# Spreading one row of scalars over 128 partitions: TensorE transposes against two DMA hops

## The chip, the cores and the metric

The kernel runs on one core of a Trainium2 chip. The metric is the device time of one execution in microseconds; the kernel before takes 571.8 us (median of 3 runs, 571.37 to 571.92). "PE" is TensorE, "DVE" VectorE, "ACT" ScalarE, "SP" the queue engine that issues nearly all DMAs, "us" microseconds.

## What is computed

A decoder layer on 256 tokens of width 2048: a gated mixer of 8 differential-attention heads and 8 block-sparse heads, then cross-attention into a memory of 256 rows, each behind an RMSNorm and with a residual. Cut to what the change touches:

```
h = rmsnorm(x, norm_mix_g)                 # x * r_x * gain, r_x = rsqrt(mean(x^2) + eps), one per token
proj = h @ w_in                            # 2048 x 8192
lam = exp(sum(lq1 * lk1)) - exp(sum(lq2 * lk2)) + 0.2
logits = (q . k) * scale + alibi           # per head, causal
attn = softmax(logits of map 0) - lam * softmax(logits of map 1)    # differential heads
```

The kernel multiplies with the raw x (times the gain) and puts r_x in afterwards. For queries r_x is one value per partition (a token is a partition), so it is a column. Keys stand transposed, with tokens along the free axis, so they need r_x as a row of 256 values, the same on all 128 partitions: that is the tile r_row. In the same way -lambda, a single number, must stand on every partition: that is neg_lam.

## The kernel before

The input projection runs as 8 windows, one for each pair of heads, of 16 "halves" (n = 0 to 15). A half is 256 rows of a 512-column slab of weights: SP loads it (two DMAs of 256 KB, L466; 8 buffers, so the load of half h + 8 waits until DVE is done with half h), ACT rounds it to a high part (L898), DVE subtracts to get a low part (L1229, two halves ahead of PE), and PE does 12 matmuls of 512 columns with them (L629 to L631). Halves 0 to 7 give the queries and keys of the pair, halves 8 to 15 its values and gates. The attention of a pair is woven into this stream by the number n in the loops of every engine, and each engine does its instructions strictly in the order written.

Around the change, in window 0: at n = 8 ACT copies the finished query and key projection to SBUF (L1003) and SP turns it with two DMA transposes (L485, issued behind the first two loads of the next window). At n = 8 DVE also works out r_x (L1449 to L1276), spreads it along the free axis (L1452, the tile r_rows) and then works on lambda; lambda is finished at n = 9 (L1471). At n = 10 PE transposes r_rows (L741, two transposes) and multiplies a matrix of ones with the column that holds -lambda in its partition 0 and zeros elsewhere (L745). At n = 11 DVE copies both results out of PSUM (L1476, L1477). At n = 12 DVE first makes the low part of half 14 (L1229), then scales the keys by r_row (L1295) and makes the low parts of queries (L1301) and keys (L1301 again), the last behind ACT's high part of the keys (L1014). PE needs all of them for the scores, which stand behind half 13 (L693 to L699).

At the very start PE runs matmuls on a tile of ones (keep_busy, L639) while the first data arrive. That tile lies in the first half of r_row.

Of the kernel before, what the change touches and what calls it, by code (L numbers as in the profile page):

```python
# [30 lines left out]
P = 128  # L31
SEQ = 256
DM = 2048
NT = SEQ // P
# [67 lines left out]
WARM_UP = (5, 2)  # L102
# [2 lines left out]
Y_TURN_AT = 6  # L105
P_TURN_AT = (10, 11)
MEM_LOAD_AT = 14


class Slots:  # L110
# [23 lines left out]
def program(nc, x, mem, norm_mix_g, w_in, lambda_q1, lambda_k1, lambda_q2, lambda_k2,  # L134
            subln_g, w_out, norm_mem_g, mem_norm_g, w_q_mem, w_kv_mem, w_o_mem, final_g, out):
    with ExitStack() as ctx:
# [3 lines left out]
        def sem(name):  # L140
            return ctx.enter_context(nc.semaphore(name))
# [18 lines left out]
        r_row = sbuf("r_row", [P, SEQ])  # L160
        alibi = sbuf("alibi", [P, 2, SEQ])
        pool = sbuf("pool", [P, 9 * COLS])
        ident = sbuf("ident", [P, P])
# [30 lines left out]
        y_sb, at = carve(pool, at, NT, 2 * P)  # L194
        junk, at = carve(pool, at, COLS)
        assert at <= 9 * COLS

        r_rows = y_sb[:, :, 0:P]

        ones = r_row[:, 0:P]  # L200
        junk_row, _ = carve(pool, 0, DM)
# [124 lines left out]
        r_x_ready = sem("r_x_ready")  # L326
        lam_steps = sem("lam_steps")
        ones_ready = sem("ones_ready")
        lam_zeroed = sem("lam_zeroed")
        lam_made = sem("lam_made")  # L330
        lam_dots = sem("lam_dots")
        lam_exps = sem("lam_exps")
        lam_ready = sem("lam_ready")
        r_rows_ready = sem("r_rows_ready")
        r_row_made = sem("r_row_made")
        r_row_ready = sem("r_row_ready")
        qk_planes_ready = sem("qk_planes_ready")
        qk_turned = [sem("qk_turned0"), sem("qk_turned1")]
        qk_merged = sem("qk_merged")
# [116 lines left out]
        def _(sp):  # L456
# [38 lines left out]
            def turns(n, j, y_too=True):  # L495

                if n == QK_TURN_AT:
                    for t in range(NT):
                        turn_qk(j - 1, t)
                if n == Y_TURN_AT and y_too:  # L500
                    turn_y(j - 2)
                if n in P_TURN_AT:
                    turn_probabilities(j - 1, n - P_TURN_AT[0])
# [25 lines left out]
            for n in range(PAIR_HALVES):  # L529
                load_pair_half(DIFF, 1, 1, n)  # L530
                turns(n, 1, False)
            with sp.Fori(2, KIND_PAIRS) as j:
                for n in range(PAIR_HALVES):
                    load_pair_half(DIFF, j, j, n)
                    turns(n, j)
# [72 lines left out]
        def _(pe):  # L608
# [26 lines left out]
            def keep_busy(count):  # L635


                with pe.Fori(0, count):
                    pe.matmul(ps[:, 2, 0:P], ones, ones, start=True, stop=True)  # L639

            def transpose_gains():

# [79 lines left out]
            def pair_window(j, kind, first=False):  # L722

                for n in range(PAIR_HALVES):
                    within = n % (2 * NG)
                    if n == 0:
                        wait(pe, qk_planes_ready, 2 * j)
                    if n == PAIR_HALVES // 2:
                        if first:
                            pe.wait_ge(gainsT_ready, 3)  # L730
                        wait(pe, v_ready, 2 * j)
                    if first and n < PAIR_HALVES // 2:
                        first_half_group(n)
                    else:
                        half_group(PAIR_HALVES * j + n, n % SPLITS, (0, 1) if n < PAIR_HALVES // 2 else (2, 3),
                                   aT_hi, aT_lo, within * (GK // 2), within == 0, within == 2 * NG - 1)
                    if first:
                        if n == 10:
                            pe.wait_ge(r_rows_ready, 1)
                            for t in range(NT):  # L740
                                m = pe.transpose(ps[:, 6, t * P:(t + 1) * P], r_rows[:, t], ident[:, :])  # L741
                            m.then_inc(r_row_made, 1)
                            pe.wait_ge(ones_ready, 1)
                            pe.wait_ge(lam_ready, 2)
                            pe.matmul(ps[:, 6, SEQ:SEQ + 1], ones, neg_lam_row[:, :], start=True, stop=True  # L745
                                      ).then_inc(lam_made, 1)
                    else:
                        attend_values(n, j - 1, WINDOW)
                    attend_scores(n, j, kind)

# [4 lines left out]
            pe.transpose(ps[:, 3, 0:KO], mix_gain[:, :], ident[0:KO, 0:KO]).then_inc(gainsT_made, 1)  # L755
            transpose_rows(0)
            transpose_rows(1)
            keep_busy(WARM_UP[1])
            pair_window(0, DIFF, True)
            with pe.Fori(1, KIND_PAIRS) as j:  # L760
                pair_window(j, DIFF)
# [460 lines left out]
        def _(dve):  # L1222
# [198 lines left out]
                rsqrt(r, ms, newton[:, 0:NT], steps, extra + 1)  # L1421

            dve.memset(ones, 1.0).then_inc(ones_ready, 1)
            dve.memset(neg_lam_row, 0.0).then_inc(lam_zeroed, 1)
            dve.wait_ge(gainsT_made, 1)
            dve.tensor_copy(gainsT[:, 0:KO], ps[:, 3, 0:KO]).then_inc(gainsT_ready, 1)
            dve.wait_ge(gainsT_ready, 1)
# [17 lines left out]
            for n in range(2 * NG, PAIR_HALVES):  # L1445
                split_lo(n + 2, n + 2)
                if n == 8:
                    dve.wait_ge(x_summed, 2 * NT)
                    dve.tensor_reduce(x_sq, x_sq2, axis=AX.X, op=ALU.add).then_inc(x_total, 1)  # L1449
                    dve.wait_ge(x_total, 1)  # L1450
                    row_rms(x_sq, x_ms, r_x, r_x_steps, 0)
                    dve.tensor_copy(r_rows, r_x.unsqueeze(2).to_broadcast([P, NT, P])).then_inc(r_rows_ready, 1)  # L1452
                    for kind in (DIFF, MOBA):
                        dve.tensor_scalar(r_q[kind.name], r_x, kind.scale, None, ALU.mult).then_inc(r_q_ready, 1)
                    dve.tensor_scalar(neg_r_x, r_x, -1.0, None, ALU.mult).then_inc(r_x_ready, 1)
                if n == 8:
                    dve.wait_ge(lam_loaded, 64)
                    for i in range(2):
                        dve.tensor_tensor(lam_prod[0:1, i], lam_in[0:1, 2 * i], lam_in[0:1, 2 * i + 1], ALU.mult
                                          ).then_inc(lam_steps, 1)  # L1460
                    for i in range(2):
                        dve.wait_ge(lam_steps, i + 1)
                        dve.tensor_reduce(lam_dot[0:1, i:i + 1], lam_prod[0:1, i], axis=AX.X, op=ALU.add
                                          ).then_inc(lam_dots, 1)
                if n == 9:
                    dve.wait_ge(lam_exps, 1)
                    dve.wait_ge(lam_zeroed, 1)
                    dve.tensor_tensor(neg_lam_row[0:1, :], lam_exp[0:1, 1:2], lam_exp[0:1, 0:1], ALU.subtract
                                      ).then_inc(lam_ready, 1)
                    dve.wait_ge(lam_ready, 1)  # L1470
                    dve.tensor_scalar(neg_lam_row[0:1, :], neg_lam_row[0:1, :], -LAM_INIT, None, ALU.add  # L1471
                                      ).then_inc(lam_ready, 1)
                if n == 11:
                    dve.wait_ge(r_row_made, 1)
                    dve.wait_ge(lam_made, 1)
                    dve.tensor_copy(r_row[:, :], ps[:, 6, 0:SEQ]).then_inc(r_row_ready, 1)  # L1476
                    dve.tensor_copy(neg_lam, ps[:, 6, SEQ:SEQ + 1]).then_inc(r_row_ready, 1)  # L1477
                    dve.wait_ge(r_row_ready, 2)
                    dve.wait_ge(r_q_ready, 2)
                attend_scores(n, 0, DIFF)  # L1480
            with dve.Fori(1, KIND_PAIRS) as j:
# [157 lines left out]
```

## Time and profile before

| | us |
|---|---|
| median of 3 runs | 571.8 |
| the profiled execution | 571.67 |
| its span | 569.9 |
| PE busy | 561.0 (98%) |
| DVE busy | 427.5 (75%) |
| ACT busy | 407.8 (72%) |
| 16 DMA engines, busy share of queue 1 | 75.5% |

The span is the time from the first to the last instruction of the profiled execution; 1.8 us of its time lie outside. PE is busy nearly all the time, so only what keeps PE waiting, or adds work to it, lengthens the run. Matmuls overlap in the pipeline: a 512-column matmul is shown with 0.39 us, but one starts every 0.23 us, so starts are compared, not durations.

### The profile page before, as it was taken

How to read it: one execution, taken by the hardware profiler on the slowest of the kernel's cores; microseconds unless marked ns; L12 is line 12 of the kernel's file. 1: busy time of each engine (PE TensorE's matmuls, PEld its weight loads, DVE VectorE, ACT ScalarE, POOL GpSimd, SP SyncE). 2: the span in 40 equal slices, each digit the busy share in tenths (PEclk: the TensorE clock that was granted, in tenths of full speed). 3: DMA queues.
4: the chain of work that ended last, by engine and by line, in shares of the span. 5: the costliest groups of instructions: out<-in, count | busy, mean ns of one | idle time of the engine just before them, and what ended most of it. 6: DMA issues, size and time to landing. Idle time of an engine off the chain costs nothing.

```text
span 569.9 us, 8636 instructions
## 1 busy us (share of the span) xinstructions
PE 561.0 (98%) x2652; PEld 467.8 (82%) x2652; DVE 427.5 (75%) x720; ACT 407.8 (72%) x653; POOL 2.1 (0%) x26
## 2 busy tenths in 40 slices
PE   8999999999999999999999999999999999999994
PEld 7888888888888888888888888888888888888884
DVE  4779768778887876866756768667568886878985
ACT  5796876967868778776784784875498796856543
POOL 1000000000000000000000000000000000000000
PEclk9999999999999999999999999999999999999998
DMA  8996768668676776885975975769799987973903
GB/s 260 353 306 227 214 180 243 181 193 237 186 232 192 198 218 185 234 230 158 250 215 157 263 206 188 221 187 302 246 227 271 262 239 197 257 230 105 258 1 147
DMA packets 151236, 123.32 MB, mean 216 GB/s; under 512 B 66809, under 2 KB 133162, under 8 KB 150698
## 3 DMA queue, kind: packets, MB, share of 16 engines
q1 hardware_dynamic: 150890, 122.47, 75.5%
q10 hardware_dynamic: 320, 0.53, 0.3%
q8 instruction: 12, 0.20, 0.1%
q14 instruction: 14, 0.11, 0.1%
HBM read 105.93 MB, written 2.10 MB: 190 GB/s over the span
## 4 chain that ended last, share of the span: by engine, by line
PE 97%; DMA 1%; DVE 1%; ACT 0%; SPq 0%; issue 0%; ACTq 0%
PE ps L629 28%; PE ps L630 28%; PE ps L631 28%; PE ps L711 2%; PE ps L693 1%; PE ps L668 1%; PE ps L672 1%; PE ps L664 1%; PE ps L868 1%; PE ps L873 1%; PE ps L869 1%; DMA xs<-in_x 1%; PE ps L651 1%; PE ps L836 0%; PE ps L696 0%; PE ps L842 0%
## 5 line engine op out<-in xcount | busy, mean ns | idle before, releaser
L1229 DVE TENSOR_TENSOR w_lo<-w_raw,w_hi 128x1024 fp32r<-128x1024 f32 x183 | 222.7, 1223 | 104.7 <-ACT w_hi L898 102.7
L898 ACT ACTIVATE w_hi<-w_raw 128x1024 fp32r<-128x1024 f32 x183 | 192.5, 1057 | 81.8 <-PE ps L631 80.7
L629 PE MATMUL ps<-w_hi,aT 128*128 128x512 f32 x540 | 211.7, 392 | 0.0
L630 PE MATMUL ps<-w_lo,aT 128*128 128x512 f32 x540 | 210.3, 389 | 0.0
L631 PE MATMUL ps<-w_hi,aT 128*128 128x512 f32 x540 | 210.1, 389 | 0.0
L631 PEld LDWEIGHTS ps<-w_hi,aT 128*128 128x128 f32 x540 | 101.4, 188 | 21.2
L629 PEld LDWEIGHTS ps<-w_hi,aT 128*128 128x128 f32 x540 | 101.4, 188 | 20.9
L630 PEld LDWEIGHTS ps<-w_lo,aT 128*128 128x128 f32 x540 | 101.4, 188 | 20.4
L629 PE MATMUL ps<-w_hi,yT_hi 128*128 128x512 f32 x144 | 56.2, 390 | 0.0
L631 PE MATMUL ps<-w_hi,yT_lo 128*128 128x512 f32 x144 | 56.0, 389 | 0.0
L630 PE MATMUL ps<-w_lo,yT_hi 128*128 128x512 f32 x144 | 56.0, 389 | 0.0
L631 PEld LDWEIGHTS ps<-w_hi,yT_lo 128*128 128x128 f32 x144 | 27.0, 188 | 5.6
L629 PEld LDWEIGHTS ps<-w_hi,yT_hi 128*128 128x128 f32 x144 | 27.0, 188 | 5.6
L630 PEld LDWEIGHTS ps<-w_lo,yT_hi 128*128 128x128 f32 x144 | 27.0, 188 | 5.5
L1286 DVE RECIPROCAL pool<-pool 128x128 f32<-128x128 f32 x32 | 30.5, 953 | 1.1
L1003 ACT ACTIVATE mems<-ps 128x1024 uint16<-128x1024 uint16 x16 | 15.5, 1020 | 17.0 <-PE ps L631 16.9
L1024 ACT ACTIVATE pool<-pool,small 128x256 f32<-128x256 f32 (+1 forms) x48 | 21.3, 444 | 7.2 <-DVE small L1321 7.2
L973 ACT ACTIVATE pool<-mems 128x1024 uint16<-128x1024 uint16 x16 | 21.7, 1359 | 0.0
L1313 DVE SCALAR_TENSOR_TENSOR pool<-ps,small,alibi 128x256 f32<-128x256 f32 (+2 forms) x32 | 15.0, 511 | 5.8 <-PE ps L699 5.8
L964 ACT ACTIVATE probT<-mems 128x768 uint16<-128x768 uint16 x16 | 16.0, 1080 | 0.0
L1038 ACT ACTIVATE mems<-pool 128x768 uint16<-128x768 uint16 x16 | 13.3, 832 | 2.9 <-DVE pool L1338 2.9
L1203 ACT ACTIVATE pool<-xs 128x512 f32<-128x512 f32 (+1 forms) x8 | 4.8, 606 | 12.0 <-DVE xs L1574 12.0
(213 smaller groups left out, 580.0 us busy)
## 6 DMA issues: line engine op xcount, KB each, us to landing
w_raw<-in_w_in SPq DMA_DIRECT2D x251, 256.0 KB, 3.2
w_raw<-in_w_out SPq DMA_DIRECT2D x64, 256.0 KB, 3.9
w_raw<-in_w_kv_mem SPq DMA_DIRECT2D x32, 256.0 KB, 4.4
w_raw<-in_w_q_mem SPq DMA_DIRECT2D x16, 256.0 KB, 3.2
w_raw<-in_w_o_mem SPq DMA_DIRECT2D x16, 256.0 KB, 3.8
mems<-in_mem SPq DMA_DIRECT2D x1, 2048.0 KB, 9.6
xs<-in_x SPq DMA_DIRECT2D x3, 512.0 KB, 6.3
w_raw<-in_w_in SPq DMA_DIRECT2D x10, 128.0 KB, 4.6
```

The source lines that it names most:

```text
L629: pe.matmul(acc, hi[:, k0 + k, tok], w_hi[:, slot, k], start=first and k == 0, stop=False)
L630: pe.matmul(acc, hi[:, k0 + k, tok], w_lo[:, slot, k], start=False, stop=False)
L631: m = pe.matmul(acc, lo[:, k0 + k, tok], w_hi[:, slot, k], start=False, stop=last and k == GK // 2 - 1)
L898: act.activation(w_hi[:, i % SPLITS], raw, ACT.Copy).then_inc(hi_made, 1)
L964: act.activation(probT[:, u].rearrange("p i q -> p (i q)").bitcast(U16) .rearrange("p (c h) -> p h c", h=2), probT_planes[:, u].rearrange( ...
L973: act.activation(qkT_sb[:, :, t * P:(t + 1) * P].bitcast(U16) .rearrange("p i (q h) -> p h i q", h=2), qkT_planes[:, t].rearrange("p (h i ...
L1003: act.activation(qk_planes[:, t].rearrange("p (h c) -> p h c", h=2), ps[:, t, :].bitcast(U16).rearrange("p (c h) -> p h c", h=2), ACT.Copy ...
L1024: m = act.activation(prob_sb[:, u, c, cols], prob_sb[:, u, c, cols], ACT.Exp, bias=neg_max[:, u, t, c:c + 1], accum_out=exp_sum[:, c, u, t ...
L1038: act.activation(prob_planes[:, u].rearrange("p (h c) -> p h c", h=2), prob_sb[:, u, 0, :].bitcast(U16).rearrange("p (c h) -> p h c", h=2) ...
L1229: dve.tensor_tensor(lo, w_raw[:, i % RAW], hi.bitcast(F32), ALU.subtract).then_inc(lo_made, 1)
L1286: dve.reciprocal(s, s).then_inc(silu_steps, 1)
L1313: dve.scalar_tensor_tensor(prob_sb[:, u, 0:kind.maps, cols], banks[:, :, cols], r[:, t:t + 1], bias, ALU.mult, ALU.add).then_inc(logits_re ...
```

## The change

Two SP-issued hops take the place of the transposes. Behind the load of half 2 of window 1, SP waits for r_x and issues two DMAs that write the 256 values of r_x, four bytes from each partition, into one line of partition 0 (r_line, in the space of y_sb). Behind the load of half 3 it issues a DMA that writes -lambda from partition 0 to all partitions, waits until the line has landed and until PE has read the ones, and issues a DMA that reads the line 128 times and writes it to the 128 partitions of r_row. DVE at n = 11 waits for both landings instead of copying from PSUM. The loop of keep_busy is written out, so that its last matmul can signal.

```diff
--- before.py
+++ after.py
@@ -105,6 +105,8 @@
 Y_TURN_AT = 6
 P_TURN_AT = (10, 11)
 MEM_LOAD_AT = 14
+R_LINE_AT = 2
+R_ROW_AT = 3
 
 
 class Slots:
@@ -195,7 +197,7 @@
         junk, at = carve(pool, at, COLS)
         assert at <= 9 * COLS
 
-        r_rows = y_sb[:, :, 0:P]
+        r_line = y_sb[0:1, 0, :]
 
         ones = r_row[:, 0:P]
         junk_row, _ = carve(pool, 0, DM)
@@ -326,14 +328,13 @@
         r_x_ready = sem("r_x_ready")
         lam_steps = sem("lam_steps")
         ones_ready = sem("ones_ready")
-        lam_zeroed = sem("lam_zeroed")
-        lam_made = sem("lam_made")
+        ones_read = sem("ones_read")
         lam_dots = sem("lam_dots")
         lam_exps = sem("lam_exps")
         lam_ready = sem("lam_ready")
-        r_rows_ready = sem("r_rows_ready")
-        r_row_made = sem("r_row_made")
-        r_row_ready = sem("r_row_ready")
+        r_line_landed = sem("r_line_landed")
+        r_row_landed = sem("r_row_landed")
+        neg_lam_landed = sem("neg_lam_landed")
         qk_planes_ready = sem("qk_planes_ready")
         qk_turned = [sem("qk_turned0"), sem("qk_turned1")]
         qk_merged = sem("qk_merged")
@@ -529,6 +530,16 @@
             for n in range(PAIR_HALVES):
                 load_pair_half(DIFF, 1, 1, n)
                 turns(n, 1, False)
+                if n == R_LINE_AT:
+                    sp.wait_ge(r_x_ready, 1)
+                    for t in range(NT):
+                        sp.dma_start(r_line[:, t * P:(t + 1) * P], r_x[:, t:t + 1]).then_inc(r_line_landed, 16)
+                if n == R_ROW_AT:
+                    sp.wait_ge(lam_ready, 2)
+                    sp.dma_start(neg_lam, neg_lam_row[0:1, :].to_broadcast([1, P])).then_inc(neg_lam_landed, 16)
+                    sp.wait_ge(ones_read, 1)
+                    sp.wait_ge(r_line_landed, 32)
+                    sp.dma_start(r_row[:, :], r_line.unsqueeze(1).to_broadcast([1, P, SEQ])).then_inc(r_row_landed, 16)
             with sp.Fori(2, KIND_PAIRS) as j:
                 for n in range(PAIR_HALVES):
                     load_pair_half(DIFF, j, j, n)
@@ -635,8 +646,9 @@
             def keep_busy(count):
 
 
-                with pe.Fori(0, count):
-                    pe.matmul(ps[:, 2, 0:P], ones, ones, start=True, stop=True)
+                for _ in range(count):
+                    m = pe.matmul(ps[:, 2, 0:P], ones, ones, start=True, stop=True)
+                return m
 
             def transpose_gains():
 
@@ -734,17 +746,7 @@
                     else:
                         half_group(PAIR_HALVES * j + n, n % SPLITS, (0, 1) if n < PAIR_HALVES // 2 else (2, 3),
                                    aT_hi, aT_lo, within * (GK // 2), within == 0, within == 2 * NG - 1)
-                    if first:
-                        if n == 10:
-                            pe.wait_ge(r_rows_ready, 1)
-                            for t in range(NT):
-                                m = pe.transpose(ps[:, 6, t * P:(t + 1) * P], r_rows[:, t], ident[:, :])
-                            m.then_inc(r_row_made, 1)
-                            pe.wait_ge(ones_ready, 1)
-                            pe.wait_ge(lam_ready, 2)
-                            pe.matmul(ps[:, 6, SEQ:SEQ + 1], ones, neg_lam_row[:, :], start=True, stop=True
-                                      ).then_inc(lam_made, 1)
-                    else:
+                    if not first:
                         attend_values(n, j - 1, WINDOW)
                     attend_scores(n, j, kind)
 
@@ -755,7 +757,7 @@
             pe.transpose(ps[:, 3, 0:KO], mix_gain[:, :], ident[0:KO, 0:KO]).then_inc(gainsT_made, 1)
             transpose_rows(0)
             transpose_rows(1)
-            keep_busy(WARM_UP[1])
+            keep_busy(WARM_UP[1]).then_inc(ones_read, 1)
             pair_window(0, DIFF, True)
             with pe.Fori(1, KIND_PAIRS) as j:
                 pair_window(j, DIFF)
@@ -1421,7 +1423,6 @@
                 rsqrt(r, ms, newton[:, 0:NT], steps, extra + 1)
 
             dve.memset(ones, 1.0).then_inc(ones_ready, 1)
-            dve.memset(neg_lam_row, 0.0).then_inc(lam_zeroed, 1)
             dve.wait_ge(gainsT_made, 1)
             dve.tensor_copy(gainsT[:, 0:KO], ps[:, 3, 0:KO]).then_inc(gainsT_ready, 1)
             dve.wait_ge(gainsT_ready, 1)
@@ -1449,7 +1450,6 @@
                     dve.tensor_reduce(x_sq, x_sq2, axis=AX.X, op=ALU.add).then_inc(x_total, 1)
                     dve.wait_ge(x_total, 1)
                     row_rms(x_sq, x_ms, r_x, r_x_steps, 0)
-                    dve.tensor_copy(r_rows, r_x.unsqueeze(2).to_broadcast([P, NT, P])).then_inc(r_rows_ready, 1)
                     for kind in (DIFF, MOBA):
                         dve.tensor_scalar(r_q[kind.name], r_x, kind.scale, None, ALU.mult).then_inc(r_q_ready, 1)
                     dve.tensor_scalar(neg_r_x, r_x, -1.0, None, ALU.mult).then_inc(r_x_ready, 1)
@@ -1464,18 +1464,14 @@
                                           ).then_inc(lam_dots, 1)
                 if n == 9:
                     dve.wait_ge(lam_exps, 1)
-                    dve.wait_ge(lam_zeroed, 1)
                     dve.tensor_tensor(neg_lam_row[0:1, :], lam_exp[0:1, 1:2], lam_exp[0:1, 0:1], ALU.subtract
                                       ).then_inc(lam_ready, 1)
                     dve.wait_ge(lam_ready, 1)
                     dve.tensor_scalar(neg_lam_row[0:1, :], neg_lam_row[0:1, :], -LAM_INIT, None, ALU.add
                                       ).then_inc(lam_ready, 1)
                 if n == 11:
-                    dve.wait_ge(r_row_made, 1)
-                    dve.wait_ge(lam_made, 1)
-                    dve.tensor_copy(r_row[:, :], ps[:, 6, 0:SEQ]).then_inc(r_row_ready, 1)
-                    dve.tensor_copy(neg_lam, ps[:, 6, SEQ:SEQ + 1]).then_inc(r_row_ready, 1)
-                    dve.wait_ge(r_row_ready, 2)
+                    dve.wait_ge(r_row_landed, 16)
+                    dve.wait_ge(neg_lam_landed, 16)
                     dve.wait_ge(r_q_ready, 2)
                 attend_scores(n, 0, DIFF)
             with dve.Fori(1, KIND_PAIRS) as j:
```

On SP, after the two transposes of the query and key projection, where the loads of window 1 (L466, L467 in the new numbering) go on; before:

```order
L485 DMA_TRANSPOSE mems<-mems 128x8x128 [waits qk_planes_ready] x2
L466 DMA w_raw<-in_w_in 128x2x256 [waits lo_made]
L466 DMA w_raw<-in_w_in 128x2x256
L466 DMA w_raw<-in_w_in 128x2x256 [waits lo_made]
L466 DMA w_raw<-in_w_in 128x2x256
```

And the same place now:

```order
L486 DMA_TRANSPOSE mems<-mems 128x8x128 [waits qk_planes_ready] x2
L467 DMA w_raw<-in_w_in 128x2x256 [waits lo_made]
L467 DMA w_raw<-in_w_in 128x2x256
L536 DMA pool<-small 1x128x1 [waits r_x_ready]
L536 DMA pool<-small 1x128x1
L467 DMA w_raw<-in_w_in 128x2x256 [waits lo_made]
L467 DMA w_raw<-in_w_in 128x2x256
L539 DMA small<-small 128x1x1 [waits lam_ready]
L542 DMA r_row<-pool 128x1x256 [waits r_line_landed,ones_read]
L467 DMA w_raw<-in_w_in 128x2x256 [waits lo_made]
```

Four DMAs have come between the loads, and the last of them has a wait for the landing of the first two; the next load stands behind it.

On DVE, at n = 9 to 12 of window 0 (small holds -lambda, pool the queries and keys), before:

```order
L1471 TENSOR_SCALAR small<-small 1x1 [waits lam_ready]
L1229 TENSOR_TENSOR w_lo<-w_raw,w_hi 128x1024 [waits hi_made] x2
L1476 COPY r_row<-ps 128x256 [waits lam_made,r_row_made]
L1477 COPY small<-ps 128x1
L1229 TENSOR_TENSOR w_lo<-w_raw,w_hi 128x1024 [waits hi_made,r_q_ready,r_row_ready]
L1295 TENSOR_TENSOR pool<-pool,r_row 128x512 [waits qk_merged]
```

And now:

```order
L1470 TENSOR_SCALAR small<-small 1x1 [waits lam_ready]
L1231 TENSOR_TENSOR w_lo<-w_raw,w_hi 128x1024 [waits hi_made] x2
L1231 TENSOR_TENSOR w_lo<-w_raw,w_hi 128x1024 [waits r_q_ready,hi_made,neg_lam_landed,r_row_landed]
L1297 TENSOR_TENSOR pool<-pool,r_row 128x512 [waits qk_merged]
L1303 TENSOR_TENSOR qT_lo<-pool,qT_hi 128x512 [waits qkT_hi_ready]
```

The two copies are gone, and the low part of half 14 now stands behind the landings.

On PE, between half 10 and half 11 of window 0, before:

```order
L631 MATMUL ps<-w_hi,aT 128x512
L741 MATMUL ps<-ident,pool 128x128 [waits r_rows_ready]
L741 MATMUL ps<-ident,pool 128x128
L745 MATMUL ps<-small,r_row 128x1 [waits lam_ready,ones_ready]
L629 MATMUL ps<-w_hi,aT 128x512 [waits lo_made]
```

And now:

```order
L641 MATMUL ps<-w_lo,aT 128x512
L642 MATMUL ps<-w_hi,aT 128x512
L640 MATMUL ps<-w_hi,aT 128x512 [waits lo_made]
L641 MATMUL ps<-w_lo,aT 128x512
L642 MATMUL ps<-w_hi,aT 128x512
```

The halves follow each other with nothing between.

## Rows read from the trace of the kernel before

**Rows 1.** The page's shares of the chain that ended last, by engine

```profile
PE 97%; DMA 1%; DVE 1%; ACT 0%; SPq 0%; issue 0%; ACTq 0%
```

**Rows 2.** Waits of PE, whole span: us in total, times, longest

```profile
PE ps L639 <- DVE r_row L1423: 1.1, 1, 1.1
PE ps L664 <- ACT w_hi L915: 0.3, 1, 0.3
PE ps L651 <- DMA xs<-in_x: 0.2, 1, 0.2
```

**Rows 3.** Chain in order of time, 38 to 50 us: start, us, what

```profile
39.55 0.23 PE ps L631
39.79 0.22 PE ps L741 x2
...
40.12 0.34 PE ps L629
...
42.98 0.23 PE ps L629
...
48.42 0.55 PE ps L693 x6
```

**Rows 4.** Timeline of DVE, 38 to 50 us: start, us, instruction [idle before]

```profile
38.78 0.14 DVE L1471 TENSOR_SCALAR small<-small 1x1 f32<-1x1 f32 x1
...
42.85 0.42 DVE L1476 COPY r_row<-ps 128x256 f32<-128x256 f32 x1
...
43.97 1.22 DVE L1229 TENSOR_TENSOR w_lo<-w_raw,w_hi 128x1024 fp32r<-128x1024 f32 x1 [0.63 <-ACT w_hi L898]
45.11 0.68 DVE L1295 TENSOR_TENSOR pool<-pool,r_row 128x512 f32<-128x512 f32 x1
...
46.49 0.69 DVE L1301 TENSOR_TENSOR kT_parts<-pool,kT_parts 128x512 fp32r<-128x512 f32 x1
47.44 2.36 DVE L1229 TENSOR_TENSOR w_lo<-w_raw,w_hi 128x1024 fp32r<-128x1024 f32 x2 [0.26 <-ACT w_hi L898]
```

**Rows 5.** Timeline of SP, 38 to 40.3 us: start, time to issue

```profile
38.07 1.09 SPq L466 DMA_DIRECT2D w_raw<-in_w_in  x2
...
39.20 0.98 SPq L466 DMA_DIRECT2D w_raw<-in_w_in  x2
```

**Rows 6.** Line L466, the two loads issued at 39.2 and 39.7: issue, landing

```profile
L466 SPq DMA_DIRECT2D w_raw<-in_w_in x2: 469/469/469, 39.2 to 39.7; - x2
...
DMA to landing us min/median/max: 3.7/4.0/4.3
```

**Rows 7.** DMA issues of the whole span: KB each, median us to landing

```profile
w_raw<-in_final_g SPq DMA_DIRECT2D x1, 1024.0 KB, 6.8
...
out<-mems SPq DMA_DIRECT2D x2, 128.0 KB, 2.5
...
mix_gain<-in_norm_mix_g ACTq DMA_DIRECT2D x1, 8.0 KB, 1.9
```

**Rows 8.** Windows: length, busy PE, PEld, DVE, ACT, POOL, PE clock, DMA share, GB/s

```profile
557.00:558.00 1.00, 1.00 (x6) 0.84 (x5) 0.80 (x2) 0.06 (x1) 0.00 (x0) 1.00 1.09 451
...
564.50:565.00 0.50, 0.00 (x0) 0.00 (x0) 0.46 (x3) 0.24 (x1) 0.00 (x0) 0.72 0.00 0
565.00:570.00 5.00, 0.00 (x0) 0.00 (x0) 0.84 (x3) 1.09 (x2) 0.00 (x0) 0.50 0.58 210
```

**Rows 9.** Timeline of PE: its last matmuls, and the start

```profile
562.07 0.64 PE L873 MATMUL ps<-w_hi,cT_lo 128*128 128x256 f32 x4
...
1.13 2.53 PE L639 MATMUL ps<-r_row 128*128 128x128 f32 x10 [1.13 <-DVE r_row L1423]
...
3.90 1.11 PE L651 MATMUL ps<-ident,xs 128*128 128x128 f32 x4
...
5.82 0.70 PE L664 MATMUL ps<-w_hi,aT 128*128 128x512 f32 x2 [0.34 <-ACT w_hi L915]
...
17.30 1.03 PE L651 MATMUL ps<-ident,xs 128*128 128x128 f32 x8
```

## The prediction

> **What bounds the kernel now.** I read the chain that ended last first: 97% of it is PE [rows 1]. Then PE's waits: in the whole span it waits three times, 1.6 us in all, and all three are over by 8 us [rows 2]. From there to its last matmul PE never stands still. So the change can help by taking instructions off PE, and it can hurt by making PE wait where it does not now; DVE, ACT and the DMA queue count only through such a wait. I therefore looked next at the chain in order of time where window 0 spreads its scalars [rows 3], at what DVE does there [rows 4], at when SP can issue [rows 5] and at how long DMAs take to land [rows 6, 7].
>
> One measurement can tell a change of about 0.2%, here 1.14 us, from none. Below, "same" means within that.
>
> **What is removed.** PE loses two transposes and the small matmul. They start at 39.79; 12 matmuls after the first one behind them (40.12) PE is at 42.98. The pace of undisturbed matmuls is (48.42 - 42.98) / 24 = 0.227 us, so without the three PE would be at 39.55 + 13 x 0.227 = 42.50. They cost 0.48 us, and since PE is the chain, that is the full gain. DVE loses its two copies out of PSUM, which begin at 42.85, but it then idles 0.63 us for ACT's high part of half 14 anyway [rows 4], so they were hidden and their going gives nothing. The spreading copy at n = 8 and the memset at the start go too; DVE waits for ACT behind both, so they give nothing either.
>
> The warm-up loop that is written out changes instructions that PE runs while it waits for x: the first transposes of x cannot start before x lands, and PE waits again for x and for ACT after them [rows 2]. Its matmuls follow each other at the array's pace (10 records in 2.53 us [rows 9]), so nothing is gained inside the loop; a gain of a tenth of a us would end in the same wait for x. I take zero; both ends are within 0.1 us.
>
> **What is added, and where it sits.** The wait on the landings stands on DVE before the low part of half 14 (now at 43.97). Call S the time at which that subtraction starts. Behind it are the scaling of the keys (S + 1.14), and the low part of the keys, which started at 46.49 and took 0.69, so ends at S + 3.21 [rows 4]. PE starts the scores at once after that, say S + 3.3. Now S = 43.97, the operands are there at 47.3 and PE gets to the scores at 48.42: 1.1 us to spare. With 0.48 us taken off PE it gets there at 47.94. So PE does not wait if S is at most 44.6, the change breaks even at S = 45.1, and each us beyond is a us of the run. Behind that DVE has to make the low parts of halves 15 and 16; they start at 47.44 as a pair of 1.2 us each, and PE needs the first only after the scores and half 14, some 4 us after 48.42. PE is later by almost as much as DVE, so this cover holds and nothing is added there. On SP the next load waits for the landing of the line, some 2 us; the weights it brings are used 8 halves (over 20 us) later, so that is covered too.
>
> **When do the landings come?** SP has issued half 2 of window 1 by 39.16 [rows 5]; r_x is ready by then, since lambda, which is worked on after it, is done at 38.92 [rows 4]. Each issue takes 0.47 to 0.5 us. The two DMAs of the line go out at 39.2 and 39.7, the load of half 3 at 40.2 and 40.7, -lambda at 41.2, and SP is free to issue the row at 41.6 at the earliest. Two loads issued at exactly 39.2 and 39.7 before landed after 3.7 and 4.3 us [rows 6]; the shortest landing of the trace is 1.9 us [rows 7]. So the line is there between 41.6 and 44.0. Its own bytes are few, where each of those loads had 256 KB (0.7 us at the 350 GB/s of the stream) and the second had the first ahead: 4.3 - 1.4 is 2.9, and the 256 pieces of four bytes may take a few tenths. I take 3.3 us, landing at 43.0.
>
> The row then moves 128 KB inside SBUF. A store of 128 KB took 2.5 us, of which 0.3 to 0.4 us is data at the pace of all 16 engines, so about 2.1 us are fixed [rows 7]; the load issued before it adds perhaps 0.3. What remains is the data itself, and here the ends lie far apart. Every one of the 128 reads of 1 KB is of the same partition, and no row shows such a transfer.
> - If the 16 engines read it side by side, the data take 0.35 us. The row nearest to that is the gain vector, one row read 128 times from outside the core, 1 MB in 6.8 us with other loads ahead: repeating a source is not slow in itself [rows 7]. Then S = 43.0 + 2.1 + 0.3 + 0.35 = 45.8 (45 to 47 with a crowded queue).
> - If one partition gives no more than one engine's share, the data take 16 times as long. The fastest us in which data were read out of SBUF moved 451 GB/s, over 128 partitions, or 28.2 GB/s for a sixteenth [rows 8]; 131,072 bytes at that rate are 4.65 us. Then S = 43.0 + 2.1 + 0.3 + 4.65 = 50.05.
>
> I take the second. The transfer reads SBUF, as the store does, and the store's rate was reached with every partition giving a little; the gain vector was read from memory outside, which says nothing about one partition of SBUF.
>
> The Trainium skill has a rule for this, "SBUF — State Buffer", section "Door 1: The DMA port swizzle": partitions reach the DMA engines through 16 ports, eight partitions to a port, and a transfer confined to one port was measured at 27.6 GB/s. By that the 131,072 bytes would take 4.75 us, an estimate from the page that falls beside the 4.65 us worked out from the rows; no run here shows it yet.
>
> With S = 50.05 the scores start at 53.35 where they started at 48.42: +4.93 us, the 0.48 us already in it. PE then stands still from 47.94 to 53.35, 5.4 us.
>
> **The clock.** The last matmuls end at 562.71 [rows 9]. The granted clock was still 1.00 until 564.5, 0.72 over the next half us and 0.50 from 565 [rows 8]: it fell from 2.4 to 1.2 GHz at 564.7, two us after PE stopped. A stop of 5.4 us should make it fall too. What the slow level costs afterwards, the start shows: four transposes of x took 1.11 us at 3.90 and eight took 1.03 us at 17.30, half the pace, and by 5.82 the 512-column matmuls ran at full pace [rows 9], so slow running lasted from 1.13 to about 5. Half of such a stretch of 3.5 to 4 us is lost, less where part of it falls in the stop: between 0.8 and 2.0 us, I take 1.6.
>
> **Sum.** 571.67 (the profiled execution's own time, 0.13 below the median) + 4.93 + 1.6 = 578.2 us, 1.1% slower.
>
> **Rivals.**
> - The clock holds through the stop: 571.67 + 4.93 = 576.6. For it: the time of the fall is known from one place only. Against it: that place had a stop of two us, this one has 5.4.
> - One partition serves all engines at once. S = 45.8, scores at 49.1, +0.7 us: 572.4, and 573.6 if both landings meet a crowded queue (S = 47). This is the wait in its small form: PE stops for a us and a half and the clock stays. For it: the gain vector's row. Against it: no read of one partition in the trace.
> - Not slower: both hops land as in a quiet queue. Line at 41.6, row issued then and landed 2.5 us later, at 44.1. S is under 44.6, PE never waits, and the 0.48 us stay: 571.2. The point from which it decides is S = 45.1. For it: the 1.9 and 2.5 us of [rows 7]. Against it: the loads at the same moment took 3.7 and 4.3.
> - The small pieces are dear: the 256 four-byte writes, all to one partition, go one after the other and the line lands 2 us later than taken. This adds its 2 us to the first number: 580.2.
>
> **Chances.** The forecast (serial reads, clock falls) 0.53; serial reads with the clock held 0.12; the small pieces dear as well 0.07; side-by-side reads 0.22; both hops quiet 0.06. The first three, and a third of the fourth (S above 46.2), are slower by over 0.2%: 0.80. The rest of the fourth and most of the fifth are within it, 0.17. Faster would need 1.14 us where PE can give back only 0.48; I leave 0.03 for what I have not seen. The range runs from 572.2, which takes in most of the fourth case, to 580.0; the forecast's own would be 576.3 to 579.5.
>
> **What would show it.** In the profile after: the row's DMA issued at about 43 and landing 7 us later (2.5 to 3 if the rival is right); SP's next load behind it at about 43.5; DVE idle from 42.85 to about 50, released by that DMA; PE idle for 5 us before the first scores, released by DVE; the PE clock at 0.5 somewhere in 50 to 57 and matmul starts 0.45 us apart there; everything after at the old pace, with no wait on PE in windows 1 to 7. A landing under 3 us, or no gap on PE ahead of the scores, makes the forecast wrong; a gap with the clock at 1.00 behind it makes only its last term wrong.

## The result, and the profile after

| | before | after |
|---|---|---|
| median | 571.83 us (4 runs) | 580.09 us (4 runs, 579.51 to 580.64) |
| the profiled execution | 571.67 | 580.64 |
| its span | 569.9 | 578.8 |

The ratio is 1.0145, 95% interval 1.0133 to 1.0157: 8.3 us slower, where 6.5 were forecast and the range ended at 580.0. The way and the mechanism were as forecast; the size was short.

PE's waits in the whole span (us in total, times, longest), which answer to [rows 2]:

```profile
PE ps L705 <- DVE kT_parts L1303: 6.8, 1, 6.8
PE ps L650 <- DVE r_row L1425: 1.1, 1, 1.1
```

There is one new wait, and it is the one ahead of the first scores. The chain of window 0 in order of time (start, us, what) answers to [rows 3]:

```profile
38.58 0.57 SPq L467
...
39.71 0.59 SPq L536
...
40.34 4.64 DMA pool<-small
...
45.04 6.41 DMA r_row<-pool
...
51.47 1.22 DVE w_lo L1231
52.70 0.61 DVE pool L1297
...
53.33 0.64 ACT kT_parts L1016
...
54.00 0.70 DVE kT_parts L1303
...
54.74 1.01 PE ps L705 x4
...
57.14 0.72 PE ps L640
57.86 0.43 PE ps L641
...
60.42 0.35 PE ps L641
60.77 0.23 PE ps L642
```

Before, only PE stood here. Now the chain runs through SP, the line's DMA, the row's DMA, DVE, ACT and DVE again until PE has its scores at 54.74, where it began them at 48.42 [rows 3]: 6.32 us. Behind that, matmuls start 0.43 us apart until about 60.6, then 0.23. The issues of the new DMAs (KB each, us to landing; [rows 7] has those of before):

```profile
r_row<-pool SPq DMA_DIRECT2D x1, 128.0 KB, 6.4
...
pool<-small SPq DMA_DIRECT2D x2, 0.5 KB, 3.7
...
small<-small SPq DMA_DIRECT2D x1, 0.5 KB, 4.3
```

And the same stretch in windows, with the PE clock in the third column from the right, then DMA share and GB/s ([rows 8]):

```profile
48.00:49.00 1.00, 0.00 (x0) 0.00 (x0) 0.00 (x0) 0.00 (x0) 0.00 (x0) 1.00 0.84 28
49.00:50.00 1.00, 0.00 (x0) 0.00 (x0) 0.00 (x0) 0.00 (x0) 0.00 (x0) 1.00 0.90 30
50.00:50.50 0.50, 0.00 (x0) 0.00 (x0) 0.00 (x0) 0.00 (x0) 0.00 (x0) 0.81 0.62 41
50.50:51.00 0.50, 0.00 (x0) 0.00 (x0) 0.00 (x0) 0.00 (x0) 0.00 (x0) 0.50 0.75 201
...
60.00:60.50 0.50, 0.50 (x2) 0.40 (x2) 0.50 (x1) 0.50 (x4) 0.00 (x0) 0.50 0.88 301
60.50:61.00 0.50, 0.50 (x3) 0.40 (x3) 0.50 (x2) 0.50 (x4) 0.00 (x0) 0.94 0.88 299
```

Two things are to be seen. While the row moves, the 16 DMA engines are 84 to 90% busy and carry 28 to 30 GB/s, where a us of loads alone carries about 300 to 350 (327 in the us from 43 to 44 of this run): they all seem to wait for something narrow. And the clock goes from 2.4 to 1.2 GHz at about 50.3, 2.4 us after PE stopped at 47.9, and comes back only at about 60.5, 5.8 us after PE went on.

What the clock cost can be read by laying the two chains beside each other. Of before:

```profile
49.74 0.43 PE ps L629
50.17 0.24 PE ps L630
50.41 0.23 PE ps L631
```

Its scores took 49.74 - 48.42 = 1.32 us, those of after 57.14 - 54.74 = 2.40: 1.08 us more. The next 8 matmuls took 0.43 + 0.24 + 6 x 0.23 = 2.05 us before and 60.77 - 57.14 = 3.63 after: 1.58 more. Together 2.66 us, which is the price of the clock in this execution, and 6.32 + 2.66 = 8.98 is the difference of the two profiled executions, 580.64 - 571.67 = 8.97. No time is left to explain elsewhere.

### The profile page after: what moved, and what is told of

It is laid out like the page before. It is cut to its first block, busy times and chain, and to the rows that moved or that the text cites. A ratio compares the mean times of both kernels' runs of the same rounds, so it can differ in the third digit from the quotient of the medians.

```text
span 578.8 us, 8611 instructions
## 1 busy us (share of the span) xinstructions
PE 563.6 (97%) x2648; PEld 469.9 (81%) x2648; DVE 426.9 (74%) x716; ACT 408.1 (71%) x653; POOL 2.1 (0%) x26
## 4 chain that ended last, share of the span: by engine, by line
PE 92%; DMA 3%; ACT 2%; SPq 1%; DVE 1%; issue 1%; ACTq 0%
PE ps L640 27%; PE ps L641 27%; PE ps L642 27%; PE ps L723 2%; PE ps L705 1%; DMA r_row<-pool 1%; PE ps L875 1%; PE ps L871 1%; PE ps L870 1%; DMA xs<-in_x 1%; DMA pool<-small 1%; PE ps L680 1%; PE ps L676 1%; PE ps L684 1%; ACT pool L1094 1%
## 5 line engine op out<-in xcount | busy, mean ns | idle before, releaser
L1016 ACT ACTIVATE kT_parts<-pool 128x512 fp32r<-128x512 f32 x8 | 5.1, 632 | 14.9 <-DVE pool L1297 14.9
```

## The experiments

All times below stand beside runs of the kernel before on the same chip, 571.8 to 571.9 us.

**The source of the row.** The last hop reads all 128 partitions in place of one:

```diff
-sp.dma_start(r_row[:, :], r_line.unsqueeze(1).to_broadcast([1, P, SEQ]))
+sp.dma_start(r_row[:, :], xs[:, 0, 0:SEQ])
```

> The changed kernel, but the last hop (128 KB into r_row) reads 1 KB from each of the 128 partitions of xs instead of 128 times the one line in partition 0, so r_row holds other values; same bytes, same pieces, same place in the queue. Theory A (one partition gives only about 28 GB/s): the landing falls from 6.4 us to about 2.5, DVE starts the low part of half 14 at about 47.6 instead of 51.5, the scores begin at 50.9 instead of 54.7: 3.9 us less, so 576.2 us, or 573.5 if the stop of 2.9 us no longer makes the clock fall. Rival (a hop of 128 KB inside SBUF takes this long whatever it reads, or it stands behind the weights in the queue): landing 6.4 us, 580.1 us.

Measured 575.17 us (573.49 to 575.54), ratio 1.006 (1.0044 to 1.0075). Its DMA issues, and DVE behind the landing (start, us, [idle before]):

```profile
r_row<-xs SPq DMA_DIRECT2D x1, 128.0 KB, 2.0
```

```profile
46.92 1.23 DVE L1231 TENSOR_TENSOR w_lo<-w_raw,w_hi 128x1024 fp32r<-128x1024 f32 x1 [2.77 <-DMA r_row<-xs]
```

The same bytes at the same place land in 2.0 us instead of 6.4. The 4.4 us between them are the source's. The 2.0 us hold some data too, 0.29 us at the 451 GB/s of [rows 8], so one partition takes about 4.7 us for its 131,072 bytes, 28 GB/s, and 1.7 us of a landing are fixed. Both are estimates from these rows. The profiled execution is the fastest of the four. Its stop was only 0.9 us where 2.9 were expected, since PE came to the scores at 49.3 and not at 47.9 (more on that at the end), and the clock stayed at 1.00. The other three runs took 574.8 to 575.5 us at a mean granted clock of 0.993 to 0.995, where the profiled one had 0.998, so the clock probably fell in them; their traces were not taken.

**Partition or port?** Four DMAs of 32 KB, from four neighbouring partitions or from four that lie four apart:

```diff
+for q, src in enumerate((0, 1, 2, 3)):        # the other kernel: (0, 4, 8, 12)
+    sp.dma_start(r_row[q * 32:(q + 1) * 32, :], xs[src:src + 1, 0, 0:SEQ].unsqueeze(1).to_broadcast([1, 32, SEQ]))
```

> The changed kernel, but r_row is written by four DMAs of 32 KB, each of which reads one row 32 times, from partitions 0, 1, 2 and 3 of xs (r_row holds other values). Theory B (what gives only 28 GB/s is a port that neighbouring partitions share): the 128 KB still pass one port, the last of the four lands about 6.4 us after the first is issued, DVE goes on at about 51.5, about 580 us. Rival (the limit is the single partition, each of four partitions gives its own 28 GB/s): issued until 47, the last lands at about 49, DVE goes on 2.5 us earlier than in the changed kernel, about 577.5 us.

> As the run with partitions 0 to 3, but the four DMAs read partitions 0, 4, 8 and 12 of xs. Theory B (ports shared by neighbours) and its rival (single partition) both say that the four now run side by side: the last lands at about 49, about 577.5 us; only if this one is as slow as the one with neighbours is the cost of a repeated row something else, such as the number of reads or the pieces of 1 KB: 580 us.

Measured 580.70 us with neighbours and 577.84 with the others (2 runs each; intervals of the ratios 1.0134 to 1.0174 and 1.0083 to 1.0125). Line of the four DMAs in the kernel with neighbours:

```profile
L543 SPq DMA_DIRECT2D r_row<-xs x4: 590/592/602, 45.4 to 47.3; - x4
...
DMA to landing us min/median/max: 3.3/4.2/4.5
```

And in the other:

```profile
L543 SPq DMA_DIRECT2D r_row<-xs x4: 590/592/602, 46.0 to 47.9; - x4
...
DMA to landing us min/median/max: 2.7/2.7/2.8
```

With partitions 0 to 3 the landings come later and later (3.3 to 4.5 us), DVE went on 6.4 us after the first issue, exactly as with a single partition, and a us in the middle carries 29 GB/s. With 0, 4, 8 and 12 each lands 2.7 us after its issue, DVE went on 4.7 us after the first issue, and what is left is SP's four issues one behind the other. The time, 577.84, is near the 577.5 expected, but the last landing came at 50.7 and not at 49: the DMAs ahead of the row went out later in this execution (its first issue at 46.0), and the clock cost less. So the narrow thing is shared by neighbouring partitions and is not the partition itself. That is what the Trainium skill states ("SBUF — State Buffer", "Door 1: The DMA port swizzle": partitions 0 to 3 were measured there at 27.6 GB/s, and partitions four apart lie on different ports); the traces agree, for reads that repeat one row too.

**The line.** One piece of 512 bytes in place of 128 of four bytes, from the same partition:

```diff
-sp.dma_start(r_line[:, t * P:(t + 1) * P], r_x[:, t:t + 1])
+sp.dma_start(r_line[:, t * P:(t + 1) * P], xs[0:1, t, 0:P])
```

> The changed kernel, but each of the two DMAs of the line copies 512 contiguous bytes of xs inside partition 0, one piece instead of 128 pieces of four bytes (r_row holds other values). Theory C (half of the 4.6 us to the landing of the second is the pieces, half the queue): landing at about 3 us, row issued at about 43.5, 578.5 us. Rival (it is all place in the queue): landing 4.6 us, 580.1 us.

Measured 579.02 us (2 runs), ratio 1.0125 (1.0104 to 1.0145). The second of the two DMAs landed after 3.6 us instead of 4.6. That does not price the pieces, though: the same DMA with its four-byte pieces, behind the same issues of SP, took 3.66 us in the kernel that reads 128 partitions, 3.94 and 4.25 in two kernels below (the later wait, the filled stop), and 4.40 and 4.45 in the two with four sources. So the pieces cost between 0.1 and 1.1 us, and two runs with one trace do not say where between; neither the theory's half nor its rival is shown. SP then waited only 0.2 us for the line (2.3 before), because its own issues ahead of the row ended at 44.0. The row went out 0.75 us earlier; of the 1.6 us between the two profiled executions (579.04 and 580.64) that is one half, and the other is the clock, which here came back at 58.1 and not at 60.6.

The line issued by ACT, in a queue of its own:

```diff
+act.wait_ge(r_x_ready, 1)                                     # at n = 9, behind the exponentials of lambda
+act.dma_start(r_line[:, t * P:(t + 1) * P], r_x[:, t:t + 1])   # t = 0, 1; gone from SP
```

> The changed kernel, with the two DMAs of the line issued by ACT at n = 9, so in ACT's own ring of each DMA engine, instead of by SP. Theory A (on SP the line stood behind the loads and transposes ahead of it in the ring): issued at about 38 and 38.6, each lands in 2 to 2.5 us, SP is not held up by it and issues the row at about 41.5; DVE goes on at 48, 3.5 us earlier; 576.6 us, or 574 if the clock holds. Rival (the four-byte pieces are dear, all into one partition): the landing is still about 4.6 us, row at 43.3, DVE on at 49.8, 578.4 us.

Measured 576.97 us (576.17 to 577.99), ratio 1.0095 (1.008 to 1.0111). Its chain:

```profile
37.82 0.36 ACTq L1118
...
38.22 3.30 DMA pool<-small
...
41.57 6.54 DMA r_row<-pool
...
48.13 1.23 DVE w_lo L1230
```

DVE went on at 48.1, as the first theory said, but the reason is mixed. The landing took 3.3 us (3.7 to 4.6 in the kernels that issue it on SP) and not the 2 to 2.5 expected of a queue without loads in it, and the larger gain is that the line is issued 2.1 us earlier (38.22 for 40.34), since SP is busy with transposes and a load until then. Why it takes 3.3 us in a queue of its own, no run shows. The clock did not hold: it fell at 51.8, when PE, after a stop of 3.2 us, had gone on at 51.4, and was back at 55.2. Of the 4.5 us that the profiled execution (576.17) takes more than the one of before, 2.98 are the later scores (51.40 for 48.42), and the 1.5 that remain are the clock's.

**Where the wait stands.** DVE waits behind the low part of half 14:

```diff
-if n == 11: dve.wait_ge(r_row_landed, 16); dve.wait_ge(neg_lam_landed, 16)
+if n == 12: dve.wait_ge(r_row_landed, 16)      # ahead of the keys' scaling; neg_lam_landed ahead of window 1
```

> The changed kernel, with DVE's wait for r_row behind the low part of half 14 instead of ahead of it, right before the keys are scaled, and the wait for -lambda ahead of window 1. Theory A (every us of DVE between the landing and the scores is a us of the run): DVE makes the low part of half 14 while it would wait, the chain from landing to scores is 2.1 us instead of 3.3, PE's stop is 1.15 us shorter, 578.9 us. Rival (something else, such as ACT's high part of the keys or the weights held up on SP, would end last): 580.1 us.

Measured 578.16 us (577.7 to 578.83), ratio 1.0111 (1.0094 to 1.0128), 1.9 us under the changed kernel where 1.2 were expected. Its trace shows why. It is 2.45 us shorter than that of the changed kernel: 0.88 come from a row that was issued earlier (44.16 for 45.04), 1.13 are the edit's (the scores begin 2.14 us behind the end of the wait and not 3.27), and the 0.4 that are left are the clock, which came back at 57.7. The wait cost the run what DVE had to do behind it, not only the landing.

**The clock.** PE is given work while it waits:

```diff
+if first and n == 13:
+    for _ in range(27):
+        pe.matmul(ps[:, 6, 0:P], ident[:, :], ident[:, :], start=True, stop=True)
```

> The changed kernel, with 27 fp32 matmuls of 128 columns on the identity put between half 13 and the scores of window 0, into a PSUM bank that the scores overwrite; they fill about 6 us of the time in which PE waits. Theory A (2.7 of the 8.3 us are the clock, which falls in the stop and comes back 6 us after it): the granted clock stays at 1.00, matmuls behind the scores start 0.23 us apart, about 577.4 us. Rival (the slow matmuls behind the stop come from the operands or the DMA catching up): the clock or the pace is as low as before, 580.1 us.

Measured 577.90 us (577.15 to 578.6), ratio 1.0105 (1.009 to 1.0121). The scores began at 54.53 as in the changed kernel (54.74), but the clock never fell:

```profile
50.00:52.00 2.00, 2.00 (x20) 2.00 (x20) 0.74 (x1) 0.00 (x0) 0.00 (x0) 1.00 0.96 291
52.00:54.00 2.00, 2.00 (x19) 1.93 (x18) 1.91 (x4) 0.88 (x2) 0.00 (x0) 1.00 0.87 277
54.00:56.00 2.00, 1.58 (x23) 1.39 (x22) 1.75 (x3) 2.00 (x3) 0.00 (x0) 1.00 0.67 226
```

Useless matmuls took 2.2 us off the run, 2.8 between the profiled executions (577.86 for 580.64), of which 0.2 are scores that began earlier. The fall of the clock was 2.2 to 2.6 us of the loss. What is left is the wait: the scores begin 6.11 us later than before, and the profiled execution is 6.19 longer.

**Lambda alone.** The kernel before, with only -lambda sent by DMA:

```diff
-pe.matmul(ps[:, 6, SEQ:SEQ + 1], ones, neg_lam_row[:, :], start=True, stop=True)
+sp.dma_start(neg_lam, neg_lam_row[0:1, :].to_broadcast([1, P]))   # waited for ahead of window 1
```

> The kernel before with one part of the change: -lambda goes to all partitions by DMA, the row of r_x stays with TensorE's transposes; DVE waits for the landing only ahead of window 1, where it is first read. Theory A: a landing of 4.3 us is covered by 10 us, PE loses one small matmul and nothing waits: 571.6 to 571.8 us, not to be told from before (571.8). Rival (a small DMA among the loads holds up the weights, or the wait is not covered): over 573 us.

Measured 571.69 us (11 runs), ratio 1.000 (0.9991 to 1.001). It landed after 4.1 us and nobody waited: this half of the change is harmless, and worth nothing that can be measured.

**Nothing is spread.** DVE fills both tiles with constants, so r_x is missing in the keys and lambda is not the input's:

```diff
+dve.memset(r_row[:, :], 1.0)
+dve.memset(neg_lam, -0.5)
```

> The changed kernel without any spreading: DVE fills r_row with ones and neg_lam with -0.5 where it copied them out of PSUM before, so r_x is left out of the keys and lambda is not the input's. It measures the gain term of the sum by itself. Theory A (PE gives back the 0.48 us of the two transposes and the small matmul, and no more): 571.35 us. Rival (a TensorE-only interruption costs more or less than its place in the chain says): 570.5 us or less, or 571.8 us.

Measured 571.75 us (11 runs), ratio 0.9998 (0.9989 to 1.0007). The interval holds both 0.48 us of gain and none, so the gain was not measured. Its trace shows the halves following each other 0.23 us apart across the place of the old transposes, with no interruption, but PE had reached its full pace later at the start and came to the scores at the time of before (48.46 for 48.42). The changed kernel's own trace shows the gain better: both begin their 512-column matmuls at 5.82, and there PE is done with half 13 at 47.93, where it was at 48.42 before, 0.49 us later. The gain is far below the 8 us it was traded for.

**The best form of the change.** The line goes to partition 0 by ACT and to partition 64 by GpSimd, and each feeds half of r_row in a queue of its own; the wait stands late:

```diff
+pool_e.dma_start(r_line2[:, t * P:(t + 1) * P], r_x[:, t:t + 1])                    # r_line2 = y_sb[64:65, 0, :]
+pool_e.dma_start(r_row[64:P, :], r_line2.unsqueeze(1).to_broadcast([1, 64, SEQ]))
+sp.dma_start(r_row[0:64, :], r_line.unsqueeze(1).to_broadcast([1, 64, SEQ]))         # behind the load of half 2
```

> The best version of the change that the runs so far point to: the line of r_x is written twice, to partition 0 from ACT's queue and to partition 64 from GpSimd's; the upper 64 partitions of r_row are read from partition 0 by SP, the lower 64 from partition 64 by GpSimd, in queues of their own; -lambda comes a load later; DVE waits for r_row only before it scales the keys. Theory B (28 GB/s for each of two ports side by side): line landed at 41.5, each half of the row takes 1.8 us and 2.3 us of data, r_row is there at about 46, scores possible at 48.1 where PE arrives at 47.9: about 571.5 us, not to be told from before. Rival (the halves still pass one after the other, or GpSimd's queue is slow): r_row at 48 or later, 573.5 us or more.

Measured 574.22 us (572.29 to 575.16), ratio 1.0042 (1.0029 to 1.0055). Its DMA issues:

```profile
r_row<-pool SPq DMA_DIRECT2D x1, 64.0 KB, 4.1
...
r_row<-pool POOLq DMA_DIRECT2D x1, 64.0 KB, 4.3
```

Side by side the halves land in 4.1 and 4.3 us where the whole took 6.4, as two ports say. DVE scaled the keys at 46.9 and PE stopped for 1.4 us in the profiled execution, which at 572.29 is the fastest of the six. The 571.5 expected were reached in none: in the profiled execution the later line landed at 41.9 and the second half of the row at 46.8, not at 41.5 and 46. The rival's time came nearer, but its mechanism (one half after the other) did not happen. With that stop filled:

```diff
+if first and n == 13:
+    for _ in range(6):
+        pe.matmul(ps[:, 6, 0:P], ident[:, :], ident[:, :], start=True, stop=True)
```

> The version with two ports, with 6 fp32 matmuls of 128 columns on the identity between half 13 and the scores of window 0 (about 1.4 us of PE, as long as its stop there in the profiled execution). That version's profile has a stop of 1.4 us with the clock at 1.00 and takes 572.3 us, but its other runs take up to 575.2. Theory D (in those the stop is long enough for the clock to fall, and the fall costs some 2 us): with the stop filled the runs come down and together, 572.3 to 573.3 us. Rival (the landings themselves come up to 3 us later in those runs, and PE waits for them): the spread stays, median about 574.2 us.

Measured 573.06 us (11 runs, 572.35 to 574.1), ratio 1.0024 (1.0015 to 1.0033). The runs came together as the first theory said, so in the slower runs without the filling the clock is the likely cause. Their mean granted clock goes with that (0.997 for 572.29, 0.996 for 573.11 and 573.84, 0.995 for the three from 574.61 on), but the kernel before also shows 0.995 to 0.998 at nearly equal times, and their traces were not taken, so it is argued and not shown. Even this form is slower than the kernel before. Two DMA hops, over 4 us each here, do not fit between r_x at 36.7 and the scaling of the keys at 45.1.

## Why the prediction was right and where it was short

- **The gain of 0.48 us**: right in the trace, where PE is done with half 13 at 47.93 for the 47.94 expected; in the times no run could measure so little.
- **The hidden parts** (DVE's copies, the loads held up on SP, the halves behind the scores): right. There is no other new wait on PE, and the chains account for all of the difference.
- **The wait on DVE and its lever** (S + 3.3): right. S was 51.47 and the scores began at 54.74, 3.27 later.
- **The row's data** (4.65 us, one partition as wide as one engine's share): right in size; 6.4 us to the landing for the 7.05 taken, since the fixed part was about 1.7 and not 2.4 (2.03 us to the landing from 128 partitions, less 0.29 of data); 4.65 + 1.74 is 6.39. This error of 0.6 us went the other way and hid as much of the miss. The reason given was half right: it is the port of neighbouring partitions, not the partition. The rival of side-by-side reads is refuted, and the row that spoke for it, a vector read 128 times from outside the core, says nothing about SBUF's ports.
- **The line's landing** is a term that was mis-sized: "I take 3.3 us, landing at 43.0". It landed at 45.0. The second DMA went out at 40.34 in place of 39.7 (the transposes ahead took SP 3.27 us to issue for 2.74, and each DMA of the line 0.59 for 0.47), and it took 4.64 us. The same DMA took 3.66 to 4.64 us in the six kernels that issue it there, so 3.3 was too low for all of them, and the latest landing that the working allowed, 44.0, was passed in every one of the six (44.1 to 45.9). How much of it is the four-byte pieces stays open: between 0.1 and 1.1 us, where I had allowed "a few tenths". The transposes took 2.7 to 3.9 us to issue in the runs, though nothing ahead of them on SP was changed, so a working from the one trace of before could not fix this part. The rival of dear pieces put 2 us on the landing and came out at 580.2. That much did come, but the pieces can be at most about half of it, so that its number is near the measured one is in good part luck. With the row 0.6 us quicker, S came out 1.4 us later.
- **The clock** is the other: it fell as forecast (2.4 us after the stop), but "between 0.8 and 2.0 us, I take 1.6" became 2.66. I took the length of the slow stretch from the start of the program and let part of it fall in the stop; in fact PE ran slow for 5.8 us after it went on. That is the long end of what the runs show: 3.8 to 5.8 us. The start was also a weak row for it, since its granted clock is shown at 1.00. The clock-holds rival is refuted.

The two terms make 1.39 + 1.06 = 2.45 us, and 578.2 + 2.45 = 580.65 is the profiled execution. The median, 580.09, lies 0.55 under it; the landing of the line and the return of the clock both differ from run to run by more than that.

## What to carry to other kernels

Before a broadcast is given to DMA, ask from how many groups of partitions it reads: bytes by 28 GB/s for each group, on top of about 1.7 us (the second DMA of the line, only 0.5 KB among the loads, took 3.3 to 4.6 us here), and 0.5 to 0.6 us for every issue on a queue that has other work. The groups tried here are partitions 0 to 3 against 0, 4, 8 and 12, and 0 with 64. When an engine that was never idle is made to wait, price the wait and the clock behind it apart: here the later scores were about seven tenths of the loss and the clock three tenths, and 27 useless matmuls bought most of that back. And compare the gain at stake (0.5 us) with the slack at the place (1.1 us) before adding two landings to it.

## What the runs showed that I had not expected

- The clock needed 5.8 us of work after the stop to come back, where it fell 2.4 us into it. Neither is fixed: in the six traces with a stop of 3.2 to 7.2 us it fell 2.4 to 4.9 us after PE stopped and came back 3.8 to 5.8 us after PE went on, and stops of 0.9 and 1.4 us left it at 1.00. In the run from partitions four apart, where the stop was 4.4 us, it fell at about 54.5, half a us after PE had gone on, and was back at about 57.9. A gap that ends before the clock has fallen can still be paid for behind it. Its windows:

```profile
54.00:54.50 0.50, 0.50 (x8) 0.50 (x10) 0.34 (x1) 0.50 (x2) 0.00 (x0) 0.96 0.96 283
54.50:55.00 0.50, 0.50 (x8) 0.50 (x6) 0.50 (x1) 0.50 (x2) 0.00 (x0) 0.50 0.96 334
...
57.50:58.00 0.50, 0.50 (x3) 0.40 (x2) 0.50 (x3) 0.00 (x0) 0.00 (x0) 0.63 1.09 381
```

- The time at which PE first reaches full pace at the start of the program differs from run to run: the first 512-column matmuls of the nothing-spread kernel started 0.43 us apart until about 8 us, those of before were fast from 5.8. That is part of why PE came to the scores up to 1.6 us later in some traces than in the changed kernel's (49.6 in the run from partitions four apart, 49.3 in the one from 128 partitions, for 47.9), and it sets how much can be told apart here. The profile shows the granted clock at 1.00 all through these slow starts, so that they are the clock's doing is not shown.
- A DMA of 0.5 KB in 4-byte pieces takes SP longer to issue (0.59 us) than one of 256 KB (0.47). It isn't the pieces: as one piece of 512 bytes it took 0.58 and 0.65 us, and 32 KB from one partition 0.59 to 0.60.
